# One weight load of the second layer takes another place in SyncE's queue, among the loads of the expert rows

## What is computed

```python
for layer in range(DEPTH):                     # 2 layers
    hn = rmsnorm(h, attn_norm[layer])
    h = h + (even_mixer if layer % 2 == 0 else odd_mixer)(hn, ...)
    h = h + hierarchical_moe(rmsnorm(h, ffn_norm[layer]), ...)
return rmsnorm(h, final_norm)

# odd_mixer begins with one projection of hn (1024 wide) to 1440 columns:
c_q, c_kv, k_pe, q_s, k_s, v_s = split_cols(hn @ w_in, [384, 256, 32, 512, 128, 128])
# hierarchical_moe: 32 experts of hidden width 256, every token goes to 2 of them
```

## Time and profile before

| what | value |
|---|---|
| time, median of 3 runs | 1120.44 us (1118.99 to 1121.47) |
| profiled execution, its own time | 1119.14 us |
| its span | 1117.2 us |
| PE busy | 1039.8 us, 93% of the span |
| mean granted TensorE clock | 0.984 |
| read from and written to HBM | 261.94 MB and 30.44 MB, 262 GB/s over the span |

### The profile page before, as it was taken

The page is one execution under the profiler, slowest core; times in us unless marked ns, Lnnn a source line. Parts: engine busy times, 40 slices in busy tenths (PEclk is TensorE's granted clock), DMA queues, the critical chain, the costliest instruction groups (busy, mean ns, idle before and its releaser), DMA issues.

```text
span 1117.2 us, 13304 instructions
## 1 busy us (share of the span) xinstructions
PE 1039.8 (93%) x5232; PEld 554.4 (50%) x5232; DVE 406.8 (36%) x1131; ACT 253.8 (23%) x669; POOL 157.1 (14%) x168
## 2 busy tenths in 40 slices
PE   5999999999998999999788998899998999999786
PEld 3344644455455555555434647536454555555442
DVE  3122720345154432233235316548126332233125
ACT  3122620245011111111012216437111111111002
POOL 2000000000101223323201000000101123322220
PEclk9999999999998999999899999999999999999898
DMA  9521207955308999999999210024534999999986
GB/s 321 218 90 69 76 2 197 221 222 189 100 38 338 352 411 412 409 411 410 410 385 359 100 75 1 10 75 156 190 113 156 353 410 412 412 411 411 411 354 227
DMA packets 80064, 277.00 MB, mean 248 GB/s; under 512 B 10537, under 2 KB 14745, under 8 KB 71291
## 3 DMA queue, kind: packets, MB, share of 16 engines
q1 hardware_dynamic: 68464, 256.56, 60.3%
q0 software_dynamic: 11536, 19.58, 5.1%
HBM read 261.94 MB, written 30.44 MB: 262 GB/s over the span
## 4 chain that ended last, share of the span: by engine, by line
PE 78%; DMA 11%; DVE 4%; issue 3%; ACT 2%; SPq 1%; POOL 0%; POOLq 0%; DVEq 0%; ACTq 0%
PE bank L1024 16%; PE bank L811 13%; PE bank L901 10%; PE bank L823 9%; PE bank L1037 8%; DMA W<-in_moe_w_up 7%; PE bank L842 5%; PE bank L1013 3%; PE bank L853 3%; PE bank L869 2%; PE bank L1172 2%; PE bank L1031 2%; PE bank L935 1%; DMA expert_rows<-K,small 1%; ACT P L1297 1%
## 5 line engine op out<-in xcount | busy, mean ns | idle before, releaser
L1024 PE MATMUL bank<-W,K 128*64 128x256 f32 x640 | 152.9, 394 | 21.6 <-DMA W<-in_moe_w_up 19.9
L1025 PE MATMUL bank<-W,K 128*64 128x256 f32 x640 | 152.9, 394 | 0.0
L811 PE MATMUL bank<-hnT,W 128*128 128x512 f32 x336 | 145.1, 593 | 0.8 <-ACT hnT L1263 0.8
L1694 DVE SCALAR_TENSOR_TENSOR PT<-bank,small,PT 64x256 f32<-64x256 f32 x64 | 31.4, 491 | 253.5 <-ACT PT L1333 253.5
L1024 PEld LDWEIGHTS bank<-W,K 128*64 128x64 f32 x640 | 87.1, 141 | 70.3 <-DMA W<-in_moe_w_up 21.6
L643 POOL DMA_INDIRECT K<-rows,small x64 | 65.6, 1025 | 399.3 <-DVE K L1714 275.3
L811 PEld LDWEIGHTS bank<-hnT,W 128*128 128x128 f32 x336 | 63.5, 190 | 80.5 <-issue 79.5
L1037 PE MATMUL bank<-D,PT 128*64 128x512 f32 x208 | 100.3, 604 | 0.7 <-ACT PT L1337 0.7
L1039 PE MATMUL bank<-D,PT 128*64 128x512 f32 x208 | 100.3, 604 | 0.0
L1025 PEld LDWEIGHTS bank<-W,K 128*64 128x64 f32 x640 | 87.1, 141 | 0.0
L1333 ACT ACTIVATE PT<-bank,small 64x256 f32<-64x256 f32 x64 | 29.9, 467 | 236.5 <-PE bank L1025 233.9
(11 more groups left out here) (249 smaller groups left out, 1508.7 us busy)
## 6 DMA issues: line engine op xcount, KB each, us to landing
D<-in_moe_w_down SPq DMA_DIRECT2D x52, 1024.0 KB
W<-in_moe_w_gate SPq DMA_DIRECT2D x40, 1024.0 KB
W<-in_moe_w_up SPq DMA_DIRECT2D x40, 1024.0 KB
hnT<-in_moe_w_down SPq DMA_DIRECT2D x12, 1024.0 KB
W<-in_e_w_in SPq DMA_DIRECT2D x5, 2048.0 KB
expert_rows<-K SPq DMA_DIRECT2D x2, 4096.0 KB, 34.6
Q<-in_moe_w_gate SPq DMA_DIRECT2D x6, 1024.0 KB
Q<-in_moe_w_up SPq DMA_DIRECT2D x6, 1024.0 KB
```

What stands on the lines that cost most here:

```text
L811: last = nc.tensor.matmul(b[:, :], w[:, k, 128 * fb:128 * fb + 128], hnT[:, k, :], start=(k == 0), stop=(k == KD - 1))
L1024: nc.tensor.matmul(bank[2 + e2][0:64, 0:256], xt, w[0][:, at:at + 256], start=first, stop=end)
L1025: last = nc.tensor.matmul(bank[2 + e2][64:128, 0:256], xt, w[1][:, at:at + 256], start=first, stop=end)
```

## The change

The load of `oT` leaves its place between the last expert load and `load_expert_rows`. In layer 0, `load_expert_rows` now issues it itself, after the row pairs of chunks 0, 1 and 2 and before that of chunk 3. The wait for `s_gu` to reach 22 goes with it; `load_expert_rows` already waits for 24. No byte, no matmul and no other order is changed.

```diff
                 for c in range(C):
+                    if lay == 0 and c == 3:
+                        load_cols("oT", odd_tile[0], owin_v, 0, 512)
                     sp.dma_start(h[:, c, :], y[128 * c:128 * c + 128, 0:DM]).then_inc(s_yld[c], 16)
                     sp.dma_start(y_in[c], y[128 * c:128 * c + 128, DM:2 * DM]).then_inc(s_yld[c], 16)
...
             experts(0)
-            sp.wait_ge(s_gu, 22)
-            load_cols("oT", odd_tile[0], owin_v, 0, 512)
             load_expert_rows(0)
```

## The result

The changed kernel takes 1123.62 us (median of 19 runs, 1119.13 to 1143.82) against 1120.04 us of the kernel before in the same sessions (19 runs). The ratio is 1.0028 with a 95% interval from 1.0016 to 1.0039: slower by 3.1 us, between 1.8 and 4.4. The highest of the 19 runs, 1143.82, had a mean granted clock of 0.94, against 0.98 to 0.99 in the others, and is left out of the ratio. The forecast was 1121.6, in a range from 1118.3 to 1124.3. So the time lies in the range and on the forecast side, but the loss of 3.1 us is two and a half times the 1.2 us that were forecast (the 2.2 us of the repetition are 1.9 times that).

The account below looks back on a forecast made before the run. PE was taken to set the pace from latent_rows(0) on, its start held by row pair 0's transfer. Landing of oT +0.85 and clock +0.35 gave +1.2 us on 1120.44, so 1121.6, range 1118.3 to 1124.3.

Parts of the forecast that it names:

- The wait that ends last: At the layer seam, the transfer of row pair 0 is the last wait to end; DVE idles 4.38 us for it.
- Row pair 0 sooner by 2.3 us, and only that: Without oT ahead, row pair 0 lands 5.5 us after SP's first row issue instead of 7.8.
- PE ready at 7.9 us behind that, 2.65 us earlier than before: PE could start latent_rows(0) at 586.9, 7.9 us after row pair 0, if its weights were there.
- oT lands at 16.9 us after the first row issue and takes over as the wait: oT, seventh in SP's queue, lands at 590.4, so latent_rows(0) starts 0.85 us later than before.
- The estimate of 14.0 us: By the Trainium skill's figures, oT lands at 587.5 and latent_rows(0) starts 2.05 us earlier than before.
- The clock, +0.35 us: Slow PE clock behind the gap at latent_rows(0) costs 2.1 us after the change against 1.74 before.
- What stays hidden: Row pair 3 and W2, queued behind oT, land later but are needed later; 3 us of delay costs nothing.
- The sum: Whole kernel: +0.85 us from oT's landing and +0.35 from the clock make +1.2 us, a median of 1121.6.
- The rival of the slower side: At the seam, oT lands at 592.6 and the clock's price reaches 2.6 us: +3.9 us, 1124.3; chance 25%.
- The full gain: At the seam, oT lands by 586.9 and PE starts 2.65 us earlier: 1117.8; chance 7%.

Follow-up runs that it names:

- e1: The changed kernel run once more with no edit, against the kernel before: ratio 1.0020 (1.0003 to 1.0037).
- e4: Half of oT left in the old place, the other half sent behind row pair 1, against the kernel before: ratio 0.9999.
- e9: oT in halves behind row pairs 1 and 2, second wait inside latent_rows(0), DVE norms chunk 2 before add_row(3), against the kernel before: ratio 1.0013.
- e11: oT behind row pair 1, one filler matmul ahead of and one behind the transposes, DVE norms chunk 2 before add_row(3), against the kernel before: ratio 1.0037.
- e6: Only one eighth of oT loaded, in the old place, so later numbers are wrong, against the kernel before: ratio 0.9998.
- e3: All of oT sent behind row pairs 0 and 1, ahead of pairs 2 and 3, against the kernel before: ratio 1.0006.
- e5: All of oT sent behind all four row pairs, against the kernel before: ratio 1.0043.
- e2: The kernel before run again as if it were a change, no edit: ratio 0.9992 (0.9974 to 1.0010).
- e7: The changed kernel plus six filler matmuls in PE's gaps ahead of latent_rows(0), against the kernel before: ratio 1.0014.
- e8: oT behind row pairs 0 and 1, one filler matmul ahead of the transposes and two behind, against the kernel before: ratio 1.0023.
- e10: The kernel before plus four filler matmuls in PE's gaps at the seam, against the kernel before: ratio 0.9985 (0.9964 to 1.0006).
- e12: The kernel before with its four filler matmuls, run a second time, against the kernel before: ratio 0.9993 (0.9977 to 1.0009).

## Why the prediction was right, and where it was off

*The wait that ends last.* The forecast took it to be the transfer of row pair 0. The chain of waits of the kernel before goes through row pair 1, whose second half is issued at 575.21:

```profile
575.21 9.49 DMA hnT<-expert_rows
```

DVE adds chunk 1's halves before it norms chunk 0, so PE's transposes wait for both pairs. In before pair 1 was 3.05 us behind, and this made 0.51 us of wait; below it made more.

*Row pair 0 sooner by 2.3 us, and only that.* Right: 5.7 us after the first row issue, and 5.3 us in e1, against a forecast of 5.5. The comparison with layer 1 gave it, and the DMA share of 0.21 ahead of the rows came as read from the earlier trace rows.

*PE ready at 7.9 us behind that, 2.65 us earlier than before.* Right for the transposes in the first profile (5.7 us behind row pair 0, forecast 5.85). In e1, e4 to e9 and e11 row pair 1 came 3.4 to 4.4 us behind pair 0, where I had taken 3.05, and in e1 the transposes came 1.3 us later behind pair 0 than forecast. Since oT was later still, that cost nothing in the changed kernel; it did in e6.

*oT lands at 16.9 us after the first row issue and takes over as the wait.* Right in kind, shown by e1, e3 and e5, and in size to 0.3 us in the first profile (592.86 - 575.69 = 17.2), but 18.0 in e1. The start of latent_rows(0) moved by 1.7 us on the mean of two profiles each (30.8 against 29.1 from E), forecast 0.85. So this term of the sum was mis-sized: the landing took 0.7 us longer than forecast on the mean, and SP's first row issue came 0.3 us sooner and not 0.4. The Trainium skill, "DMA: Bandwidth & Descriptors", section "Anatomy of one DMA", gives its fit for one transfer issued by GpSimd. The estimate of 14.0 us that the prediction made from it for seven loads on SyncE's queue does not agree with the trace's 17.2.

*The clock, +0.35 us.* This step was mis-sized too, and the reason is on the side of before. I took its price before as 1.74 us from one execution. e2 shows an execution without it, so by two profiles the mean is 0.9. After, the price was 1.6 in both, a little less than the 2.1 forecast. The difference is 0.7 to 0.8 us and not 0.35. e7 shows the side of after, by taking the 1.6 us away. The side of before rests on two profiles, and the timed runs support it: the mean granted clock of the changed kernel's fast runs was 0.983 to 0.984, that of the kernel before 0.985 to 0.986, and that of e7 0.986. The Trainium skill, "TensorE: Matmul & The Clock Gate", section "HAM oscillation — how this bites in real kernels", says that waits for transfers between products let the clock drop, so that each product begins slowly; e3, e5 and e7 agree with it. But waits of 1 to 2.5 us had a fall behind them in before and e4, and none in e2.

*What stays hidden.* Right: the time from the end of latent_rows(0) to the product with W3 is 33.95 us in before, e2, after and e1 alike, by the table's sums to 0.1 us. Row pair 3 behind oT cost nothing there, and nothing in e7 either, where latent_rows(0) was fast (33.95 again). It is row pair 2 behind oT that the slow product covers, in e3, and e8 uncovers.

*The sum.* Forecast 0.85 + 0.35 = 1.2 us; the seam shows 1.7 + 0.75 = 2.5; timed were 3.1 (1.8 to 4.4) and 2.2 (0.3 to 4.1). What remains between 2.5 and the two timings is inside their intervals. The rival of the slower side had the right direction and a too large size: a landing 19 us after the first row issue and 2.6 us of slow clock were not needed. That the forecast came out in its range is thus earned in the mechanism, and in part lucky in the size: both terms were about half of what they measured. The full gain did not come: oT landed 17.2 and 18.0 us after the first row issue, where 0.2% wanted less than 587.3 - 573.5 = 13.8.

*Left open.* What half of oT ahead of the rows costs them (e4). The whole delays them by 0.7 to 2.5 us from one profile to the next, and the rows here don't separate the 16 DMA engines. And e6 and e9 have a seam 2.2 and 0.8 us shorter than before without a shorter time; their intervals are wide enough for it, and nothing more was tried.

## What to carry to other kernels

Before moving a load out of the way, look at what the queue does at that moment: a load that fills idle DMA engines in front of a wait costs less there than its length. Here 5.3 us of transfer (2.1 MB at 393 GB/s) delayed the rows by 2.3 us; once moved, it landed 5.9 us after row pair 2, which went out just ahead of it. A change of order in one queue must be followed to the second and third waiting engine, since an earlier start uncovered the next thing in line: a row pair in e8, DVE's own work in e9 and e11. And an event that comes in one execution and not in the next, like the fall of the clock behind a gap, has to be priced over several profiles of the unchanged kernel, not one.

## What the runs showed of the hardware

The last scatter's landing depends on what is queued beside it. It went out either 7.3 or 9.0 us behind E. I read its landing from SP's first row issue, which waits for it. Sent at 7.3, it had landed 6.0 to 6.3 us later in every kernel. Sent at 9.0 it took 4.3 us in e1, e5 and e9, with nothing behind the experts' weights, but 5.4 to 5.6 us in e4, e10 and e12, with all or half of oT there. So in such executions the change gives SP its first row issue about 1.2 us sooner (E + 13.2 against 14.4 to 14.6), a small gain that I had put at 0.4.

Filler matmuls in PE's gaps held the granted clock at 1.00 up to the end of latent_rows(0) in all five profiles that had them. Without them it fell to 0.50 in before, after, e1, e3, e4 and e5, and stayed at 1.00 in e2, e6 and e9. PE's gap ahead of the product was 1.9 us in e3 and 4.4 to 7.0 in after, e1 and e5, and the clock fell in all four. Fillers guard only the product behind them: in e11 the clock fell behind the next gap, and latent_rows(1) took 8.80 us. In e8 the second filler ends where the product starts, 1.1 us later than in e3. But e11, with one filler less, starts at E + 28.7 as well after 0.42 us of idling, and row pair 2 behind oT is 0.8 and 1.1 us later in e8 and e11 than in e3. So it was oT that was later there, and not the filler.
